# Two transformer blocks on one core: where the first block's squares are summed, which engine scales four filter taps, and three reordered seams

## The reference

```python
def first_block(x, ...):
    h = x
    h = h + 0.5 * swiglu_ffn(rmsnorm(h, ffn1_norm), ffn1_w_in, ffn1_w_out)
    u = rmsnorm(h, mix_norm) @ w_mix_in
    # y_conv: gated short convolution; y_gdn: gated delta rule, rmsnorm(o) * silu(z)
    h = h + concatenate([y_conv, y_gdn]) @ w_mix_out
    h = h + 0.5 * swiglu_ffn(rmsnorm(h, ffn2_norm), ffn2_w_in, ffn2_w_out)
    return rmsnorm(h, final_norm)

def second_block(x, c, positions, ...):
    h = rms_norm(x, g_pre_mix) * (1.0 + scale1) + shift1
    z = h @ w_in                      # u_glu, q_lat, kv_lat, k_r, gate_logits
    u = ua * sigmoid(ub)
    u = causal_depthwise_conv_2(u, conv_w, conv_b)      # 31 taps, 1024 channels
    y_a = silu(layer_norm(u)) @ w_conv_out
    y_b = attention(rms_norm(q_lat) @ w_uq, rms_norm(kv_lat) @ w_ukv, k_r) @ w_attn_out
    y = (g_a * y_a + g_b * y_b) @ w_out
    x = x + gate1 * rms_norm(y, g_post_mix)
    h = rms_norm(x, g_pre_mlp) * (1.0 + scale2) + shift2
    return x + gate2 * rms_norm(square(relu(h @ w_mlp_in)) @ w_mlp_out, g_post_mlp)
```

## Time and profile before

| | us |
|---|---|
| median of 3 runs | 1032.51 |
| lowest and highest | 1031.68 and 1032.97 |
| the profiled execution | 1032.48 |
| its span, first to last instruction | 1030.7 |
| busy: PE, DVE, POOL, ACT | 1015.1, 794.2, 510.5, 497.3 |

### The profile page before, as it was taken

One profiled execution on the slowest core, in us unless ns is written; L12 is line 12 of the kernel. 1 busy time (PEld: TensorE's weight loads), 2 busy tenths in 40 slices (PEclk: granted clock), 3 DMA queues, 4 the chain that ended last, 5 costly groups with the idle time before them and its releaser, 6 DMA issues.

```text
span 1030.7 us, 19098 instructions
## 1 busy us (share of the span) xinstructions
PE 1015.1 (98%) x7801; PEld 971.7 (94%) x7801; DVE 794.2 (77%) x799; ACT 497.3 (48%) x578; POOL 510.5 (50%) x300
## 2 busy tenths in 40 slices
PE   9999999999999999999999999999999999999997
PEld 7999999998999899999999999998999978899886
DVE  5777777699886678878677859998898787667764
ACT  6443433477532463443343656667576454343432
POOL 4576757510043027557577999999930004314400
PEclk9999999999999999999999999999999999999999
DMA  9968677646340256677677365672236517675641
GB/s 273 320 207 269 216 255 234 213 138 182 93 154 1 93 194 212 219 258 230 230 243 243 92 195 149 155 227 94 83 116 197 178 60 229 229 235 184 218 149 41
DMA packets 165997, 188.33 MB, mean 183 GB/s; under 512 B 10574, under 2 KB 155548, under 8 KB 165820
## 3 DMA queue, kind: packets, MB, share of 16 engines
q1 hardware_dynamic: 165580, 186.13, 56.8%
q0 software_dynamic: 192, 1.36, 0.4%
q10 hardware_dynamic: 176, 0.14, 0.1%
HBM read 186.58 MB, written 1.05 MB: 182 GB/s over the span
## 4 chain that ended last, share of the span: by engine, by line
PE 93%; DVE 4%; ACT 1%; issue 1%; DMA 0%; ACTq 0%; DVEq 0%
PE ps L1966 56%; PE ps L2010 11%; PE ps L2018 9%; PE ps L2243 2%; PE ps L1977 2%; PE ps L2189 2%; PE ps L2365 1%; PE ps L2114 1%; DVE wl L1270 1%; PE ps L2409 1%; PE ps L2058 1%; PE ps L2407 1%; PE ps L2379 1%; PE ps L2396 1%; PE ps L2048 0%
## 5 line engine op out<-in xcount | busy, mean ns | idle before, releaser
L1966 PE MATMUL ps<-xh,wh 128*128 128x256 f32 x1208 | 345.3, 286 | 3.4 <-DVE xl L1793 1.9
L1966 PE MATMUL ps<-xl,wh 128*128 128x256 f32 x1208 | 341.7, 283 | 0.0
L1966 PE MATMUL ps<-xh,wl 128*128 128x256 f32 x1208 | 341.6, 283 | 0.0
L1275 DVE TENSOR_TENSOR wl<-raw,wh 128x2048 fp32r<-128x2048 f32 x78 | 251.5, 3224 | 63.3 <-ACT wh L789 63.3
L1966 PEld LDWEIGHTS ps<-xh,wh 128*128 128x128 f32 x1208 | 231.5, 192 | 7.1 <-issue 3.9
L1966 PEld LDWEIGHTS ps<-xl,wh 128*128 128x128 f32 x1208 | 231.6, 192 | 0.5
L1966 PEld LDWEIGHTS ps<-xh,wl 128*128 128x128 f32 x1208 | 231.6, 192 | 0.0
L789 ACT ACTIVATE wh<-raw 128x2048 fp32r<-128x2048 f32 x78 | 148.9, 1911 | 148.2 <-PE ps L1966 148.2
L1270 DVE TENSOR_TENSOR wl<-raw,wh 128x2048 fp32r<-128x2048 f32 (+1 forms) x74 | 181.9, 2464 | 39.1 <-ACT wh L783 38.6
L647 POOL TENSOR_TENSOR ada_raw<-ada_raw,c_act 128x2048 f32<-128x2048 f32 x24 | 87.6, 3648 | 217.3 <-DMA ada_raw<-in_w_ada 212.2
L783 ACT ACTIVATE wh<-raw 128x2048 fp32r<-128x2048 f32 (+1 forms) x74 | 138.9, 1882 | 70.3 <-PE ps L1966 56.2
(11 more groups left out here) (407 smaller groups left out, 1840.0 us busy)
## 6 DMA issues: line engine op xcount, KB each, us to landing
raw<-in_ffn_w_in SPq DMA_DIRECT2D x43, 1024.0 KB, 7.5
ada_raw<-in_w_ada SPq DMA_DIRECT2D x24, 1024.0 KB, 5.3
raw<-in_ffn_w_out SPq DMA_DIRECT2D x22, 1024.0 KB, 5.0
raw<-in_w_in SPq DMA_DIRECT2D x18, 1024.0 KB, 5.4
raw<-in_w_mlp_in SPq DMA_DIRECT2D x16, 1024.0 KB, 5.5
raw<-in_w_mlp_out SPq DMA_DIRECT2D x16, 1024.0 KB, 4.9
raw<-in_w_mix_in SPq DMA_DIRECT2D x14, 1024.0 KB, 5.4
raw<-in_w_mix_out SPq DMA_DIRECT2D x4, 1024.0 KB, 5.3
```

The lines of the kernel that those rows point to most:

```text
L1275: dve.tensor_tensor(wl[:, s % SLOTS, :], raw[:, s % SLOTS, :], wh[:, s % SLOTS, :].bitcast(F32), ALU.subtract).then_inc(low_done, 1)
L1966: mm = pe.matmul(bank[:, m * T:(m + 1) * T], w[:, k, m * P:(m + 1) * P], r[:, k, :], start=(m == 0 and k == 0 and j == 0), stop=(k == KT - ...
```

## The change

- The first block's squares are made by ScalarE instead of GpSimd: the first pair of tiles ahead of the root L1000, the other three behind it. TensorE sums them into bank 7 between `g_stat` and glu slab 0, with two filler products instead of eleven; the column sums after glu slab 1 go. `f_kept` is copied ahead of the cast of glu slab 2, and glu slab 3 waits for it.
- `ACT_TAPS` has 15 taps of group 0 (every odd k) and 7 of group 1 instead of 12 and 6. ScalarE scales two instead of one ahead of each latent cast, and one more after `lat_sq`.
- Mixer output: slab 0's first half goes by tile ahead of the row sums. The subtraction of slab s0+17 is cut in two: one half with a semaphore of its own (`mo_half`), for which slab 2's first half waits; the other after the low parts.
- `convolve(2)` ahead of the last `attn_rest`; the subtraction of slab s+5 behind the fourth low tile of conv_out.

```diff
-ACT_TAPS = [(0, k) for k in range(1, TAPS) if k % 5 in (1, 3)] + [(1, k) for k in range(1, TAPS - SHARED_TAPS) if k % 4 == 1]
+ACT_TAPS = [(0, k) for k in range(1, TAPS) if k % 2] + [(1, k) for k in range(1, TAPS - SHARED_TAPS) if k % 7 in (1, 4)]
...
-            squares("f", "ffn2_resid", f_squares)
             pool.wait_ge(*at("ada_taken", ADA_EARLY))
...
+            def first_block_squares(b):
+                act.activation(f_squares[:, 2 * b:2 * b + 2, :], resid[:, 2 * b:2 * b + 2, :], ACT.Square).then_inc(S("f_sq"), 1)
+
+            first_block_squares(0)
             act.wait_ge(*at("g_stat", 1))
             act.activation(std[:, :], ps[6][:, 0:T], ACT.Sqrt, scale=1.0 / D, bias=eps_sq).then_inc(S("g_std"), 1)
+            for b in range(1, 4):
+                first_block_squares(b)
             for t in range(KT):
                 act.wait_ge(*at("h_f", t + 1))
                 act.activation(xh[:, t, :], scaled_input(t), ACT.Identity, bias=ada[:, t:t + 1]).then_inc(S("h_xh"), 1)
+            act.wait_ge(*at("g_rstd", 1))
+            act.wait_ge(*at("f_stat", 1))
+            act.activation(std[:, :], ps[7][:, 0:T], ACT.Copy).then_inc(S("f_kept"), 1)
             cast(FIRST["glu"] + 2)
...
-                if n == 1:
-
-                    act.wait_ge(*at("g_rstd", 1))
-                    act.wait_ge(*at("f_stat", 1))
-                    act.activation(std[:, :], ps[1][:, 0:T], ACT.Copy).then_inc(S("f_kept"), 1)
...
             for n in range(3):
-                scale_taps(1)
+                scale_taps(2)
                 cast(s + n + 3)
...
             act.activation(lat_sq, lat[:, :, :], ACT.Square).then_inc(S("lat_sq"), 1)
+            scale_taps(1)
...
             row_parts("o")
-            sub(s0 + 14 + 3)
...
+            dve.wait_ge(high_done, s0 + 14 + 3 + 1)
+            sub_part(s0 + 14 + 3, half_slab).then_inc(S("mo_half"), 1)
             dve.wait_ge(*at("gz_silu", 2))
...
+            sub_part(s0 + 14 + 3, rest_slab).then_inc(low_done, 1)
             for n in range(4):
                 s = FIRST["mix_out"] + n
...
             attn_rest(NH - 2)
+            convolve(2)
             attn_rest(NH - 1)
...
             sub(s + 4)
-            sub(s + 5)
             inverse("ln", rstd[:, :], kr_raw)
...
+                if t == 3:
+                    sub(s + 5)
                 if t == 5:
                     mix_b(3)
...
             s_out = FIRST["mix_out"]
+            wide(s_out, ps[MIX_OUT_BANKS[0]], xh, xl, "mo_xl", lambda k: k // 2 + 1, inputs=range(KT // 2), by_tile=True)
             row_sums("o", "row_of", 0, 4, ps[3], ("o_sq", 1))
-            wide(s_out, ps[MIX_OUT_BANKS[0]], xh, xl, "mo_xl", lambda k: k // 2 + 1, inputs=range(KT // 2))
...
-            wide(s_out + 2, ps[MIX_OUT_BANKS[2]], xh, xl, inputs=range(KT // 2))
+            wide(s_out + 2, ps[MIX_OUT_BANKS[2]], xh, xl, inputs=range(KT // 2), low_ready=at("mo_half", 1))
...
+            def first_block_sums(b):
+
+                pe.wait_ge(*at("f_sq", b + 1))
+                for k in (2 * b, 2 * b + 1):
+                    mm = pe.matmul(ps[7][:, 0:T], ones, f_squares[:, k, :], start=(k == 0), stop=(k == KT - 1), skip_group_check=True)
+                if b == 3:
+                    mm.then_inc(S("f_stat"), 1)
...
-            keep_busy(11, 4)
+            for b in range(4):
+                first_block_sums(b)
+                if b in (0, 3):
+                    keep_busy(1, 4)
...
+                if n == 1:
+                    pe.wait_ge(*at("f_kept", 1))
                 wide(s + 1, ps[5 + 2 * (n % 2)], xh, xl)
-                if n == 0:
-                    column_sums("f", lambda k: f_squares[:, k, :], KT, ps[1][:, 0:T], ("f_sq", 1), by_pair=True)
```

More of the change, by code:

```diff
@@ L185 @@
     "row_reads": (("gate_kept", 2), ("z_sq", 4)),
-    "row_steps": (("g_add", 3), ("gate_ready", 1), ("z_total", 2)),
+    "row_steps": (("mo_half", 1), ("g_add", 3), ("gate_ready", 1), ("z_total", 2)),
     "roots": (("n1_std", 1), ("n2_std", 1), ("qk_std", 1), ("short_std", 1), ("o_std", 1), ("n3_std", 1),
@@ L1598, in _, with sub_part @@
             row_parts("o")
-            sub(s0 + 14 + 3)
+            half_slab = slice(0, SLAB // 2)
+            rest_slab = slice(SLAB // 2, SLAB)
+            def sub_part(s, some):
+                return dve.tensor_tensor(wl[:, s % SLOTS, some], raw[:, s % SLOTS, some], wh[:, s % SLOTS, some].bitcast(F32),
+                                         ALU.subtract)
+            dve.wait_ge(high_done, s0 + 14 + 3 + 1)
+            sub_part(s0 + 14 + 3, half_slab).then_inc(S("mo_half"), 1)
             dve.wait_ge(*at("gz_silu", 2))
@@ L1953, in wide @@
             def wide(s, bank, x, y, tile_ready=None, tile_base=0, slab=None, m_tiles=2, inputs=range(KT),
-                     by_tile=False):
+                     by_tile=False, low_ready=None):
                 slab = s if slab is None else slab
-                pe.wait_ge(low_done, s + 1)
+                pe.wait_ge(*(low_ready or (low_done, s + 1)))
                 n = KT * P * m_tiles
```

## The result

The changed kernel took 1037.16 us (median of 8 runs, 1036.10 to 1037.73) against 1033.86 us before (8 runs, 1031.68 to 1034.64): ratio 1.0033, 95% interval [1.0022, 1.0044]. It is slower by some 3.4 us, where 1035.8 us and +3.35 were forecast.

A forecast was written before the change was run, and what follows sets the result against it. TensorE was taken to bound the kernel; +4.0 us at the latent sums, with the 3.95 us lead used up, and -0.65 at the third seam gave +3.35 on 1032.48, so 1035.8 us, range 1032.0 to 1039.0.

The forecast's parts named there:

- What bounds: Whole kernel: TensorE bounds it, and a saving there counts only if the engines that feed it keep up.
- the wait of the earlier trace: Before the latent sums: ScalarE already waited once, 1.75 us, on GpSimd's tap add; said to decide this case.
- Taps: Ahead of the latent sums: ScalarE's taps wait for GpSimd's adds, so the sums start 4.0 us later (3.1 to 5.0).
- rival C: After the stall before the latent sums: TensorE's clock falls, costing 1 to 3 us, total 1037.8 us; chance 0.17.
- First seam: First mixer's output: row sums move behind half a slab, the silu is late next; gain 0.4 us, 0 to 1.1.
- Second seam: Entry of the second mixer: 0.1 us (0 to 0.4), plus 3.45 us of column sums gone after glu slab 1.
- Third seam: Layer norm before conv_out: inverse 1.7 us earlier, TensorE waits 1.35 us at tile 4; gain 0.65 us, 0 to 1.7.
- Tail: End of the long convolution: GpSimd ends some 5 us ahead of TensorE's need, so nothing is late.
- Rival A: Latent sums: the taps cost nothing because GpSimd is ahead when ScalarE asks; -4.6, 1027.9 us; chance 0.13.

The follow-up runs named there:

- seven buffers: The changed kernel with seven buffers for scaled taps instead of three, four of them in kn, the work otherwise the same: 1027.18 us, ratio 0.9946.
- the old taps: The changed kernel with the tap list and tap schedule of before, the moved sums and seams staying as changed: 1031.79 us, ratio 0.9989.

## Why the prediction was right, and where it was not

**What bounds** held: TensorE's chain moved with what ScalarE fed it, and the wait of the earlier trace rows did decide the case.

**Taps.** The step was right in kind: tap 11 waited for k=17, tap 13 for k=21, with the cast, the copies and lat_sq behind them, and the tap schedule alone reproduces it. k=21 was added at 650.84 + 1.29 = 652.1, inside the 652.0 to 653.9 that were bounded and 0.8 us before the 652.9 that I took. GpSimd started on its taps only 0.1 us sooner (594.08 for 594.18) where 0.6 was said; with the 2.0 for two taps handed over, its stalls then shrank by some 2.2 us, where 0 to 1.9 were allowed. From there to lat_sq's end it took 4.6 us (652.13 to 656.77), 4.75 in the prediction, so the sums came at +3.24 instead of +4.0. TensorE's two waits are 1.6 and 4.9 us where 2.5 and 5.5 were said; k=17 too was added a little sooner, at 642.7 instead of 643 to 643.5.

**The clock** is where the forecast failed. The 4.9 us of idle were in it, their price at the clock was not: rival C stood beside it with 0.17, and C's mechanism is what happened, on top of the forecast's stall. It cost 2.9 us by the trace, at the upper end of the 1 to 3 that it was given from rows at either level. The Trainium skill's rule (TensorE: Matmul & The Clock Gate, section HAM oscillation), that long enough gaps bring the lower clock back, made C the likelier case. The runs agree for the gaps of 4.9 and 4.5 us; the falls after 2.6 and 1.64 us are beside the rule, for 1.9 us elsewhere brought none. C's mechanism belonged in the sum. One row behind its price was misread: at the kernel's start, where the fp32 product takes 0.47 us, the windows give a granted clock of 1.00, so that row is no sample of the lower level. In the stretch after the stall it is: four products in 1.71 us at a granted clock of 0.50, 0.43 each against 0.86/4 = 0.215 in before. By profile the forecast was 1.9 us too low (+5.2 against +3.35). That the medians differ by just 3.3 us, which is the forecast, is luck: the traces add up to 3.24 + 2.86 - 0.9 = 5.2, a stall sized 0.8 us too large hides part of a clock cost that the sum left out, and the rest is how the two profiled executions stand to their medians. Before itself moved from one group of runs to the next: against the medians of the experiments' groups (1032.49 to 1033.22) the same 1037.16 us is 3.9 to 4.7 us slower.

**First seam.** 0.3 us instead of 0.4, by the traces with and without it. The silu was late next, as said: in after VectorE's first product (L1616) starts at 359.18, released by ScalarE's L978, where it was released by the row spread in before. The load on SP that waits for the slab's second half left at 364.59 (364.3 said), and nothing was late for it.

**Second seam.** The 3.45 us of sums are gone from the chain. The rest is smaller than it looks. Glu slab 0 starts 0.45 us earlier, but its products follow the tiles that VectorE makes, as the prediction said; the last low tile is done at 585.66 against 585.73 in before, and at the end of slab 1 only 0.09 us are left. The o_mm products end 0.2 us later in this trace than in before, so the first two seams are worth 0.3 us there, which is the first seam's alone; the entry of the second mixer gave nothing, where 0.1 (0 to 0.4) was taken. TensorE's lead at glu slab 2 was 596.09 - 592.55 = 3.54 us instead of 3.95.

**Third seam.** 0.9 instead of 0.65. The inverse starts at 777.71, with the shift of 6.15 taken off 771.56 (771.7 said), and tile 4 waits 0.97 instead of 1.35. The start came 1.8 us earlier, as worked out; mis-sized was the wait, because tile 4 was ready 0.3 us sooner than I took it and the 24 products ahead of it ran 3.1 us and not 2.9.

**Tail.** That GpSimd's end had cover held in the changed kernel, where VectorE's last taps (L1779) start with no wait. The sentence that this cover matters only if the stall doesn't come, and then just fits, was the most useful of the part: with seven buffers VectorE waits 1.76 us for GpSimd and TensorE not at all. What I did not see is its other side: without the four taps the moved sums are worth 0.6 us, if anything, and not 3.45. The two taps of VectorE put before the last attn_rest were never undone alone, so what they are worth is open. The parts of this change are not to be added one by one: sums alone 0.9994, taps alone 1.0058 (1.0046 with seven buffers), third seam alone 0.9990, and all of them with the tap waits away 0.9946.

**Rival A** (taps free, 1027.9 us) was rejected for this kernel rightly, for k=21 was 7 us too late. But its price was nearly right: with the waits gone the time is 1027.2 to 1027.8, which is 5.3 and 5.4 us below before in their groups, where A said 4.6.

## What to carry to other kernels

An engine that makes things ahead for another, through a few buffers, must ask for a buffer no earlier in its program than the consumer frees it: count which earlier item frees the buffer and read from the trace when that one is consumed, for everything behind the wait on the same in-order engine is late by the difference. When a stall on TensorE's path is foreseen, price the clock with it; a few products that keep the array busy give that part back. And before a saving at the front is booked, ask which slower engine has to finish before the next meeting point, for the work that relieves that engine may be worth as much as the saving.

## What the runs showed of the hardware that was not expected

- How long TensorE stood idle did not alone decide whether its clock fell. 4.9, 4.5 and 2.6 us were followed by half the clock in the profiled executions; so was 1.64 us ahead of the first scores, in 8 of 11 executions going by their mean clock; but 1.9 us in front of conv_out in before, 1.77 us ahead of the row sums in before, and 1.92 us ahead of the sums of conv with the old taps were not: their windows show 1.00 throughout. By these mean clocks one and the same kernel went either way. What else decides, what the engine does around the gap or chance, no run here separates.
- The fall can cost more than the idle that brings it: 1.64 us of waiting was followed by some 10 us at half the clock, and filling it was worth 3.2 us in the mean.
- One GpSimd instruction of 4.62 us held four VectorE products with two operands back by 2.4 us (4.94 for 2.50) and left a reciprocal alone (1.75).
